# Conditioning chunks scaled and summed outside TensorE in a two-layer SSD / attention / expert kernel

## The reference

```python
cond = jax.nn.silu(c)
for l in range(DEPTH):
    mod = cond @ ada_w[l] + ada_b[l]                      # [1,1024] @ [1024, 6144]
    sh1, sc1, g1, sh2, sc2, g2 = jnp.split(mod, 6, axis=-1)
    h = modulate(rms_norm(x, mix_norm_g[l]), sh1, sc1)    # h*(1+scale)+shift
    mix = token_mixer(h, w_in[l], conv_w[l], ...)
    x = x + g1[:, None, :] * mix
    h = modulate(rms_norm(x, ffn_norm_g[l]), sh2, sc2)
    x = x + g2[:, None, :] * peer_ffn(h, peer_wq[l], peer_keys[l], peer_u[l], peer_v[l])
return rms_norm(x, final_norm_g)
```

## Time and profile before

| | |
|---|---|
| median of 3 runs | 2915.8 us (2914.14 to 2917.41) |
| the profiled execution: its time, its span | 2911.22 us, 2909.4 us |
| its granted TensorE clock | 0.995 |
| busy: PE, PEld | 2849.5 us (98%), 2665.6 us (92%) |
| busy: DVE, ACT, POOL | 2501.1 us (86%), 1446.6 us (50%), 996.6 us (34%) |
| chunks on PE | 48, as 192 products (384 rows of L1114) |

### The profile page before, as it was taken

How to read it: one execution, slowest core, us unless ns; L and a number is a source line. 1 busy time by engine, 2 the same in 40 slices (tenths; PEclk the granted TensorE clock), 3 DMA queues, 4 the chain that set the end, 5 groups by cost and what they waited for, 6 DMA issues and landing times.

```text
span 2909.4 us, 48871 instructions
## 1 busy us (share of the span) xinstructions
PE 2849.5 (98%) x17734; PEld 2665.6 (92%) x17734; DVE 2501.1 (86%) x4773; ACT 1446.6 (50%) x2309; POOL 996.6 (34%) x773
## 2 busy tenths in 40 slices
PE   6999999999999999999999999999999999999998
PEld 4777789999999999999978778999999999999998
DVE  4667789799897899999987779998999879999998
ACT  3345234488883433433353532447888633333333
POOL 1000027644443343444400000675444433443442
PEclk9999999999999999999999999999999999999999
DMA  7434647899999999999932122679999999999996
GB/s 276 170 115 185 255 148 240 304 364 380 387 334 382 346 383 383 383 377 384 380 117 73 63 69 88 199 239 354 391 377 372 348 378 357 384 379 385 377 380 251
DMA packets 252523, 854.87 MB, mean 294 GB/s; under 512 B 25568, under 2 KB 58592, under 8 KB 245728
## 3 DMA queue, kind: packets, MB, share of 16 engines
q1 hardware_dynamic: 149280, 442.23, 41.7%
q0 software_dynamic: 98496, 381.73, 35.0%
q10 hardware_dynamic: 4608, 29.36, 2.4%
HBM read 777.06 MB, written 76.15 MB: 293 GB/s over the span
## 4 chain that ended last, share of the span: by engine, by line
PE 80%; DMA 8%; DVE 7%; ACT 3%; issue 2%; SPq 0%; POOL 0%; DVEq 0%; ACTq 0%
PE banks L1049 40%; PE banks L1565 27%; DMA w_raw<-wst 4%; PE banks L1533 4%; DMA ring<-u,gidx 2%; DVE w_lo L1605 2%; PE banks L1370 2%; ACT w_hi L767 1%; PE banks L1114 1%; PE banks L1453 1%; DMA pj<-adaw 1%; DVE ring L2099 1%; PE banks L1065 1%; DVE oneh L2121 1%; DVE vacc L2111 1%
## 5 line engine op out<-in xcount | busy, mean ns | idle before, releaser
L767 ACT ACTIVATE w_hi<-w_raw 128x1024 fp32r<-128x1024 f32 x596 | 630.7, 1058 | 754.4 <-PE banks L1049 637.6
L1049 PE MATMUL banks<-hH,w_hi 128*128 128x352 f32 (+1 forms) x2528 | 865.5, 342 | 3.4 <-ACT w_hi L767 0.9
L1605 DVE TENSOR_TENSOR w_lo<-w_raw,w_hi 128x1024 fp32r<-128x1024 f32 x522 | 638.8, 1224 | 263.2 <-ACT w_hi L767 260.6
L1049 PE MATMUL banks<-hH,w_lo 128*128 128x352 f32 (+1 forms) x2528 | 845.2, 334 | 0.0
L1049 PE MATMUL banks<-hL,w_hi 128*128 128x352 f32 (+1 forms) x2528 | 844.9, 334 | 0.0
L720 POOL DMA_INDIRECT ring<-v,gidx x320 | 396.2, 1238 | 595.8 <-DVE vacc L2111 533.5
L720 POOL DMA_INDIRECT ring<-u,gidx x320 | 396.8, 1240 | 461.6 <-DVE gact L2099 444.6
L1049 PEld LDWEIGHTS banks<-hH,w_hi 128*128 128x128 f32 x2528 | 474.8, 188 | 50.1 <-issue 20.4
L1565 PE MATMUL banks<-c_lo_late,w_hi 128*128 128x352 f32 x1536 | 494.0, 322 | 0.0
L1049 PEld LDWEIGHTS banks<-hH,w_lo 128*128 128x128 f32 x2528 | 474.4, 188 | 19.5
L1049 PEld LDWEIGHTS banks<-hL,w_hi 128*128 128x128 f32 x2528 | 475.2, 188 | 17.4 <-issue 0.5
(11 more groups left out here) (347 smaller groups left out, 3991.8 us busy)
## 6 DMA issues: line engine op xcount, KB each, us to landing
w_raw<-wst SPq DMA_DIRECT2D x596, 512.0 KB, 6.5
activations<-act_out SPq DMA_DIRECT2D x124, 352.0 KB, 8.0
act_in<-activations SPq DMA_DIRECT2D x62, 704.0 KB, 8.0
gate_matrices<-stages ACTq DMA_DIRECT2D x32, 896.0 KB, 9.2
gates<-gate_matrices SPq DMA_DIRECT2D x64, 448.0 KB, 10.0
ada_buf<-adaw POOLq DMA_DIRECT2D x24, 1024.0 KB, 6.8
nrm<-adaw POOLq DMA_DIRECT2D x8, 1024.0 KB, 5.4
pj<-adaw POOLq DMA_DIRECT2D x7, 1024.0 KB, 7.6
```

The lines of the kernel that those rows point to most:

```text
L767: nc.scalar.activation(w_hi[g % 2][:, :, :].rearrange("p a b -> p (a b)"), w_raw[:, g % RAWS, :], ACT.Copy).then_inc(s_wh, 1)
L1049: last = mm(bank[s][:, 0:t.stop - t.start], a[s][:, k, :], b[:, k, t], start=(k == 0 and a is w_hi and b is hH), stop=(k == KT - 1 and a i ...
L1605: v.tensor_tensor(w_lo[g % 2][:, :, :].rearrange("p a b -> p (a b)"), w_raw[:, g % RAWS, :], w_hi[g % 2][:, :, :].rearrange("p a b -> p (a ...
```

## The change

- Chunks 8 to 23 (layer 0's sets 1 and 2) are no longer multiplied on PE. POOL multiplies each in place by its column of silu(c) (`scale_ada`, a tensor_scalar of 128x2048) and adds seven of each eight to the set's first chunk (`add_ada`, a tensor_tensor of 128x2048). When a set is summed, PE multiplies the sum once with ones (`ada_sum`): behind tile 7 and behind tile 16.
- Chunks 24 to 28 stay on PE. Chunks 29 and 30 are scaled and added on POOL.
- Chunks 31 to 47 are scaled on ACT (`activation` with a scale, 128x2048, one or two behind each query copy), and 31, 33 to 39 and 41 to 47 are added by a transfer with `accum_op=add` from SBUF to SBUF that POOL issues, each after the one before has landed. `ada_sum` stands behind scores 3, scores 9 and scores 15.
- The places of the chunks are new (`ADA_HOMES`). `last_rows` are rows 14 to 17 of `pj`, `y_tok` is the scan's output. So DVE waits for the addition of chunk 17 before it writes `y_tok` (iteration 10), and ACT for that of chunk 22 before it writes row 14 of `pj`. POOL waits for `s_dtg` (PE is done with `dt_groups`, behind tile 2) before it loads chunk 16 into `h32`, and for the sum of set 1 on PE before it loads chunk 19.

The diff, cut to its core:

```diff
+ADA_ON_PE = (KT, 0, 0, GAP_ADA, 0, 0)
+POOL_SCALED = ADA_CHUNKS + GAP_ADA + 2
+def pool_owned(n):
+    return n % KT >= ADA_ON_PE[n // KT]
+def ada_head(i):
+    return i * KT + ADA_ON_PE[i]
+ADA_TAKEN = [KT]
+for _i in range(1, 2 * ADA_SETS):
+    ADA_TAKEN.append(ADA_TAKEN[-1] + ADA_ON_PE[_i] + 1)
...
         @block.gpsimd
+            def load_ada(n, after=None):
+                if after is not None:
+                    pool.wait_ge(*ada_added(after))
+                pool.dma_start(ada_place(n), adaw[n // ADA_CHUNKS, n % ADA_CHUNKS]).then_inc(ada_sem(n)[0], 16)
+            def scale_ada(n):
+                pool.wait_ge(*ada_sem(n))
+                pool.tensor_scalar(ada_place(n), ada_place(n), tiny[:, 0, n % KT:n % KT + 1], None, ALU.mult).then_inc(s_psc, 1)
+            def add_ada(n):
+                pool.wait_ge(*ada_scaled(n))
+                pool.wait_ge(*(ada_scaled(n - 1) if n - 1 == ada_head(n // KT) else ada_added(n - 1)))
+                acc = ada_place(ada_head(n // KT))
+                if n >= POOL_SCALED:
+                    pool.dma_start(acc, ada_place(n), accum_op=ALU.add).then_inc(s_adad, 16)
+                else:
+                    pool.tensor_tensor(acc, ada_place(n), acc, ALU.add).then_inc(s_adas, 1)
+            pool.wait_ge(s_cond, 1)
+            pool.wait_ge(s_rows, 1)
+            load_ada(8)
+            pool.wait_ge(s_adat, KT)
+            load_ada(9)
+            load_ada(10)
+            scale_ada(8)
+            for n in range(9, 15):
+                scale_ada(n)
+                add_ada(n)
+                if n == 12:
                     pool.wait_ge(s_dtg, 1)
+                    load_ada(16)
+                load_ada(n + 2 if n < 14 else 17, after=n)
+            scale_ada(15)
+            add_ada(15)
+            load_ada(18, after=15)
+            scale_ada(16)
+            for n in range(17, ADA_CHUNKS):
+                scale_ada(n)
+                add_ada(n)
+                if n == 17:
+                    pool.wait_ge(s_adat, ADA_TAKEN[1])
+                    load_ada(19)
+                elif n + 2 < ADA_CHUNKS:
+                    load_ada(n + 2, after=n)
...
                 if l == 0:
                     pool.wait_ge(s_rhs, KT + 1)
+                    for n in range(ADA_CHUNKS, POOL_SCALED):
+                        load_ada(n)
+                    scale_ada(POOL_SCALED - 2)
+                    scale_ada(POOL_SCALED - 1)
+                    add_ada(POOL_SCALED - 1)
+                    load_ada(ada_head(4), after=POOL_SCALED - 1)
+                    pool.wait_ge(s_adat, ADA_TAKEN[2] + GAP_ADA)
+                    loads = [n for n in range(POOL_SCALED, 2 * ADA_CHUNKS) if n % KT != 0]
+                    for n in loads[0:ADA_SLOTS]:
+                        load_ada(n)
+                    for i, n in enumerate(loads):
+                        add_ada(n)
+                        if n == ada_head(4) + 4:
+                            pool.wait_ge(s_adat, ADA_TAKEN[3])
+                            load_ada(ada_head(5))
+                        if i + ADA_SLOTS < len(loads):
+                            load_ada(loads[i + ADA_SLOTS], after=n)
...
         @block.scalar
+                    if l == 0 and n == N_IN - 4:
+                        act.wait_ge(*ada_added(22))
                     tile_copy(n)
...
-                    if l == 0 and n in (5, 9):
-                        ada_rows(1, (n - 5) // 4)
+                    for m in scaled_in(n) if l == 0 else []:
+                        act.wait_ge(*ada_sem(m))
+                        nc.scalar.activation(ada_place(m), ada_place(m), ACT.Copy,
+                                             scale=tiny[:, 0, m % KT:m % KT + 1]).then_inc(s_asc, 1)
+                    if l == 0 and n in (5, 11):
+                        ada_rows(1, (n - 5) // 6)
...
         @block.tensor
+                def ada_sum(at, i):
+                    n = at * ADA_SETS + i
+                    if at == 0:
+                        pe.wait_ge(s_arow, i)
+                    pe.wait_ge(*ada_added(n * KT + KT - 1))
+                    acc = ada_place(ada_head(n))
+                    for j in range(ADA_GROUPS):
+                        last = mm(bank[ADA_BANK[at][i]][32 * j:32 * j + 32, :], ones[:, 0:32], acc[:, j * T:(j + 1) * T],
+                                  start=(ADA_ON_PE[n] == 0), stop=True)
                     last.then_inc(s_adat, 1)
...
-                if l == 0:
-                    ada_chunk(0, KT)
...
                 for n in range(2, N_IN):
                     project(l, n, n % 2)
-                    if l == 0 and n != KT + 1:
-                        ada_chunk(0, KT + n - 1 if n <= KT else KT + n - 2)
+                    if l == 0 and n in (7, 16):
+                        ada_sum(0, n // 7)
...
                     scores(n, n % 2)
                     if l == 0:
-                        for c in chunks_of(n):
-                            ada_chunk(1, c)
+                        if n in (3, 9):
+                            ada_sum(1, n // 9)
...
                 scores(N_Q - 1, 1)
+                if l == 0:
+                    ada_sum(1, 2)
...
         @block.vector
+                    if l == 0 and tt == 0:
+                        dve.wait_ge(*ada_added(17))
```

More of the change, by code:

```diff
@@ L170, with scaled, scaled_in @@
 PAIR_K = 5
-def chunks_of(n):
-    return [GAP_ADA + 2 * n, GAP_ADA + 2 * n + 1] if n < 4 else [n + 9]
-assert [c for n in range(N_Q - 1) for c in chunks_of(n)] == list(range(GAP_ADA, ADA_CHUNKS))
+ADA_HOMES = ("nrm", "last_rows", "y_tok", "last_rows", "y_tok", "last_rows", "y_tok", "last_rows",
+             "h32", "y_tok", "last_rows", "nrm", "last_rows", "nrm", "last_rows", "nrm",
[3 rows of a table added]
+assert KT + len(ADA_HOMES) == 2 * ADA_CHUNKS
+ADA_ON_PE = (KT, 0, 0, GAP_ADA, 0, 0)
[4 more added lines that the diff above has]
+    return i * KT + ADA_ON_PE[i]
+def scaled(n):
+    first = KT if n < POOL_SCALED else POOL_SCALED
+    return sum(pool_owned(m) for m in range(first, n + 1))
+ADA_TAKEN = [KT]
+for _i in range(1, 2 * ADA_SETS):
+    ADA_TAKEN.append(ADA_TAKEN[-1] + ADA_ON_PE[_i] + 1)
+def scaled_in(n):
+    return [m for m in range(POOL_SCALED, 2 * ADA_CHUNKS)][2 * n:2 * n + 2] if n < 2 else \
+        [m for m in range(POOL_SCALED, 2 * ADA_CHUNKS)][n + 2:n + 3]
+assert [m for n in range(N_Q - 1) for m in scaled_in(n)] == list(range(POOL_SCALED, 2 * ADA_CHUNKS))
 Y_BANK = (3, 4, 5, 2)
@@ L263, in ada_place @@
         def ada_place(n):
-            late = n - ADA_CHUNKS
-            if ADA_SLOTS <= late < GAP_ADA:
-                rows = 4 * (late - ADA_SLOTS)
-                return pj[:, rows:rows + 4, :].rearrange("p a t -> p (a t)")[:, 0:ADA_COLS]
-            if n < 3 or n >= ADA_CHUNKS:
-                return ada_buf[:, n % ADA_SLOTS, :]
+            rows = lambda r: pj[:, r:r + 4, :].rearrange("p a t -> p (a t)")[:, 0:ADA_COLS]
+            if n < 3:
+                return ada_buf[:, n, :]
             if n < 6:
@@ L451, in build @@
         s_ada0 = [sem(f"first_ada_in{k}") for k in range(KT)]
-        s_ada = [sem(f"ada_in{s}") for s in range(ADA_SLOTS)]
-        s_gap = [sem(f"gap_ada_in{s}") for s in range(GAP_ADA - ADA_SLOTS)]
+        s_ada = {h: sem(f"ada_in_{h}") for h in sorted(set(ADA_HOMES))}
         s_adat = sem("ada_chunks_multiplied")
+        s_psc = sem("ada_chunks_scaled_by_pool")
+        s_asc = sem("ada_chunks_scaled_by_act")
+        s_adas = sem("ada_chunks_added")
+        s_adad = sem("ada_chunks_added_by_dma")
         s_arow = sem("ada_rows_taken")
@@ L571, in ada_sem, with ada_scaled, ada_added @@
                 return s_ada0[n], 16
-            in_gap = lambda m: ADA_SLOTS <= m - ADA_CHUNKS < GAP_ADA
-            if in_gap(n):
-                return s_gap[n - ADA_CHUNKS - ADA_SLOTS], 16
-            s = n % ADA_SLOTS
-            return s_ada[s], 16 * len([m for m in range(s, n + 1, ADA_SLOTS) if m >= KT and not in_gap(m)])
+            home = ADA_HOMES[n - KT]
+            return s_ada[home], 16 * len([m for m in range(KT, n + 1) if ADA_HOMES[m - KT] == home])
+        def ada_scaled(n):
+            return (s_psc if n < POOL_SCALED else s_asc), scaled(n)
+        def ada_added(n):
+            heads = [ada_head(i) for i in range(1, 2 * ADA_SETS)]
+            count = lambda first: len([m for m in range(first, n + 1) if pool_owned(m) and m not in heads])
+            if n >= POOL_SCALED:
+                return s_adad, 16 * count(POOL_SCALED)
+            return s_adas, count(KT)
         block = ctx.enter_context(nc.Block())
@@ L700, in _ @@
-            for c in range(KT, ADA_CHUNKS):
-                load_ada(0, c)
+            def load_ada(n, after=None):
[5 more added lines that the diff above has]
+                pool.tensor_scalar(ada_place(n), ada_place(n), tiny[:, 0, n % KT:n % KT + 1], None, ALU.mult).then_inc(s_psc, 1)
@@ L1106, in ada_chunk @@
                     i, k = c // KT, c % KT
-                    if at == 0 and i >= 1 and k == 0:
```

(3 more changed lines are left out.)

34 lines of the change are left out of this document (15 added, 19 removed), and 3 rows, old and new, of the table ADA_HOMES.

## The result

The changed kernel takes 3110.2 us (median of four runs, 3105.5 to 3112.3) against 2916.5 us (2914.1 to 2917.4) for the kernel before on the same chip: a ratio of 1.0665, 95% interval 1.0651 to 1.068. The prediction was 2958 us with a range of 2893 to 3005: the sign was right, the size was not. The profiled execution has a span of 3103.7 us, 194.3 us more than before.

The account below looks back on a forecast made before the run. PE, busy 98% of the span, was taken to bound the kernel, with DVE at 86%. Terms -32 + 40 + 12 + 5 + 4 + 13 = +42 us on 2915.8 gave 2958 us, range 2893 to 3005.

Parts of the forecast that it names:

- What PE gains: Both layers: PE drops 14 chunks net in layer 0 (14.1 us) and 16 in layer 1 (17.9 us), -32 us.
- POOL's scaling: POOL's tensor_scalar of 128x2048 was priced at 2.8 us, range 2.4 to 4.8, from an affine_select row.
- That DVE stands still while POOL computes: Layer 0's in-projection: DVE instructions with two SBUF inputs wait for POOL's; convolution rises from 0.75 to 2 us or more.
- Up to tile 7: Layer 0's in-projection to the sum of set 1: POOL and DVE delay each other, +40 us (30 to 50).
- the upper bound: To tile 7: POOL slips in after each linked DVE instruction, DVE is late, sum of set 1 at 142 us, +50 us.
- Tile 7 to tile 16: Layer 0, set 2: part of a 45.6 us standstill shows past DVE's idle time, +12 us (0 to 25).
- Second norm: Chunks 29 and 30: two POOL scalings and an addition, 10.4 us, meet eight `hL` blocks, +5 us (0 to 10).
- PE's clock: Stalls of several us lower PE's granted clock, +4 us (0 to 10).
- Accumulating transfers: Layer 1's scores: 15 chained transfers at 5.5 to 7.2 us a link end late, +13 us (0 to 40).
- Faster: Rival: POOL's scaling and adding do not hold DVE up; -17.5 us, 2898 us, chance 0.22.
- The second: Rival: transfer links of 9 us or more are the main loss, 25 us on top, about 2983 us; chance 0.08.
- What does not move: Layer 1 (dt_groups to y_back 109.5 us before) and the expert phases should not move.

Follow-up runs that it names:

- l1_no_links: Layer 1's half of the change alone (layer1_only) with all fifteen accumulating transfers left out, each sum being its first chunk alone: 2908.3 us.
- l0_no_scaling: Layer 0's half of the change alone, without POOL's scaling, so chunks are added unscaled: 2943.5 us.
- l0_quarters: Layer 0's half of the change alone, each POOL scaling and addition of 2048 columns cut into four of 512: 2981.4 us.
- layer1_only: The changed kernel with only layer 1's half of the change; PE multiplies chunks 8 to 23 as in the kernel before: 3016.0 us, ratio 1.0345.
- both halves: The kernel before with only layer 0's part of the change, or only layer 1's: 3015.2 us (ratio 1.0342) and 3016.0 us (1.0345).

## Why the prediction was right or wrong

- **What PE gains, 32 us.** Right as far as it was seen. L1114 had 384 matmul records, 8 a chunk; after there are 104 of chunks and 40 of sums, 13 and 5. In layer 1, `l1_no_links` shows 15.2 us less in the scores where 17.9 were expected. The 14.1 us of layer 0 were not measured apart.
- **POOL's scaling, 2.8 us (range 2.4 to 4.8).** Wrong, and the first step that failed: 5.4 to 5.7 us, outside the range. The nearest row that I took, an affine_select of 128x128 less a memset, gave 1.5 ns an element; the scaling takes 2.7. That one input costs less than two was assumed, not read: it costs more (5.5 against 4.6 us). The Trainium skill (GPSIMD Engine Reference, section 4.1) calls one-input operations roughly line-rate; this trace speaks against it. In layer 0's in-projection POOL computed 154.5 us, where the prediction's prices give 16 x 2.8 + 14 x 4.8 = 112.
- **That DVE stands still while POOL computes.** Right in kind: the convolution's mean is 2013 ns, as "2 us or more" said, and `l0_no_scaling` and `l0_quarters` both move it the way a hold per POOL instruction demands. It was mis-sized by its list too: I counted only instructions with two SBUF inputs, and tensor_scalar with one added 50.5 of the 118.4 us and PE's longest wait. The sentence that brought L1682 and L1692 in stood beside the sum and not in it.
- **Up to tile 7, +40 (30 to 50).** PE takes the sum of set 1 at 164.2 us against 91.5 unhindered: +72.7. POOL had it ready at 132.3, so DVE is the late one, as the upper bound had it. DVE's standstill up to there is 72.1 us (busy 116.4 against 44.3 before). With 5.5 and 4.6 us the bound's own sum has 92 us of POOL's work in place of 66: 37 + 50 + 92 - 11 = 168 us, near the 164.2. This is an estimate made afterwards, and its closeness is partly luck, as the list without the one-input instructions is still in it. The +40 was the middle of two bounds, of which the upper one had the right path.
- **Tile 7 to tile 16, +12 (0 to 25).** From 164.2 to the second sum at 277.6 us it took 113.4 us against 74.5: +38.9. DVE's standstill is 46.4 us there (93.5 busy against 47.2), and of the assumed cover, DVE's 38.2 us of idle time before `lo`, 19.1 us are left. Dt_groups to `y_back` took 182.0 us, where the prediction named near 150.
- **Second norm, +5 (0 to 10).** 12.2 us, just outside, for three holds of 9.7 us in all. The mechanism was right; POOL's three instructions take 15.9 us where the term had 10.4, and it counted half of that.
- **PE's clock, +4 (0 to 10).** The granted clock was 0.61 and 0.82 in layer 0's in-projection and 0.83 from 392 to 572 us, against 0.87 and 1.00 before, always where PE waits for others. Up to `y_back` PE is busy 152.5 us where 143.0 less 14 chunks (14.1) would be 128.9: some 24 us more for the same work, an estimate. In `layer1_only` PE is busy 132.3 us from 298 to 508 us at 0.79, in `l1_no_links` 109.9 us from 298 to 410 at 0.98. So the term was too small if that time counts in full; but at a higher clock PE might only have waited longer for the same DVE instruction or link, and what the clock costs on its own stays open.
- **Accumulating transfers, link of 5.5 to 7.2 us, +13 (0 to 40).** Wrong, and as large as the first error: 13.45 us a link, 101.6 us lost. I priced a link by the landing of a load issued into a quieter stretch, and did not price its place: POOL issues a 1 MB load right before each. My "10 us possible" is near what a link takes when the load goes second (9.64), but by luck: it was argued from the addition's two operands, and with the load still first a plain copy takes 10.26 us a link as well.
- **The rivals.** "Faster" fell with both halves slower by 3.4%. The second, the transfer chain with links of 9 us or more, named a real mechanism and gave it 0.08; it came true together with the forecast's, with layer 0 worse and not "as forecast or milder", and its 13 + 25 = 38 us for the chain were under two fifths of the 101.6. That both main terms could be short at once, each because POOL's queue does more than I priced, was in none of the cases.
- **What does not move.** Right: layer 1's in-projection (109.5 us) and all behind it.

## What to carry to other kernels

Before work moves to POOL beside a busy VectorE, list every VectorE instruction of the stage that touches only SBUF, with one input too, and price POOL's own instruction by a row of just its kind; if there is none, the range must reach to the dearest POOL row and beyond. A chain of transfers in which each waits for the one before is priced by its length against the time it runs beside, with everything that the same queue issues ahead of each link; issue the link first, and keep chains so short that each link has more than its landing time. The same idea pays in a small dose: six links and no POOL work won 0.2% where fifteen, with POOL's work at the second norm, lost 3.4%. And where an instruction stands in its engine's queue counts as much as how long it is held: eight tensor_scalar, 3.3 us before and 22.9 after, stood ahead of one `w_lo` and cost PE its longest wait.
